# The first loads of a diffusion block in another order, the position table split, c turned with the filter's vectors

## What is computed

```
x  = x + pos_embed_2d(rows, GRID_W, D)            # table of 512 x 1024
mod = silu(c) @ w_mod + b_mod                     # 1024 -> 6144; the same with c_ctx for ctx
sh1, sc1, g1, sh2, sc2, g2 = split(mod, 6)
h  = rmsnorm(x, pre_norm1) * (1 + sc1) + sh1      # and hc from ctx with c_ctx
z  = h @ w_in                                     # Hyena group and mLSTM group
k  = hyena_filter(...)                            # 33 -> 64 -> 64 -> 64 -> 1024, sines between, times exp(-t*|delta|)
y_hy = x0 * irfft(rfft(v * x1) * rfft(k));  y_ml = two mLSTM scans, gates from h and hc
x  = x + g1 * rmsnorm([y_hy, y_ml] @ w_out)
x  = x + g2 * rmsnorm(experts(modulated rmsnorm of x))   # 16 experts, weights 3 x 8 MB each
```

## Time and profile before

| | us |
|---|---|
| median of 3 executions | 1326.48 (1326.43 to 1328.17) |
| the profiled execution | 1328.69 |
| its span, first to last instruction | 1326.6 |
| PE busy in the span | 1205.7 |
| start of hyena_tile(0) | 62.4 |
| end of hyena_tile(0) | 90.1 |
| first product of the experts | 401.8 |
| first wait of the experts for a transfer on the chain | 554.1 |

### The profile page before, as it was taken

The page is one execution under the profiler, slowest core; times in us unless marked ns, Lnnn a source line. Parts: engine busy times, 40 slices in busy tenths (PEclk is TensorE's granted clock), DMA queues, the critical chain, the costliest instruction groups (busy, mean ns, idle before and its releaser), DMA issues.

```text
span 1326.6 us, 12968 instructions
## 1 busy us (share of the span) xinstructions
PE 1205.7 (91%) x5284; PEld 500.9 (38%) x5284; DVE 351.7 (27%) x626; ACT 188.4 (14%) x392; POOL 30.6 (2%) x56
## 2 busy tenths in 40 slices
PE   5999999999989999998989798888979898897986
PEld 1444454654444353342325234232423422242332
DVE  3775729445450110210201111020102102010213
ACT  2510020134321111010101001010200101010012
POOL 2000020000000001000000000000000000000000
PEclk9999999999999999999999999999999999999999
DMA  9965410306168999999999999999999999999994
GB/s 348 387 230 222 143 64 0 127 1 253 66 258 371 390 428 429 427 427 428 428 428 429 429 428 428 428 429 429 429 427 428 429 428 429 427 429 428 428 427 168
DMA packets 44778, 455.57 MB, mean 343 GB/s; under 512 B 6193, under 2 KB 6305, under 8 KB 16971
## 3 DMA queue, kind: packets, MB, share of 16 engines
q1 hardware_dynamic: 44098, 454.95, 82.0%
q10 hardware_dynamic: 264, 0.11, 0.1%
q0 software_dynamic: 384, 0.07, 0.0%
HBM read 453.02 MB, written 2.10 MB: 343 GB/s over the span
## 4 chain that ended last, share of the span: by engine, by line
PE 59%; DMA 33%; DVE 5%; ACT 1%; issue 1%; SPq 1%; DVEq 0%; ACTq 0%
DMA ring<-in_w_exp_up 28%; PE B L1169 15%; PE B L1138 11%; PE B L720 6%; PE B L957 4%; PE B L1080 4%; PE B L841 3%; DMA ring<-in_w_exp_down 3%; PE B L899 2%; DMA ring<-in_pos 2%; PE B L1230 2%; PE B L770 2%; DVE moe L2058 1%; PE B L1151 1%; DVE yacc L2049 1%
## 5 line engine op out<-in xcount | busy, mean ns | idle before, releaser
L1138 PE MATMUL B<-ring,moe 128*64 128x512 f32 x2032 | 454.9, 596 | 75.5 <-DMA ring<-in_w_exp_up 41.5
L1138 PEld LDWEIGHTS B<-ring,moe 128*64 128x64 f32 x2032 | 139.2, 137 | 384.6 <-issue 247.5
L2058 DVE TENSOR_TENSOR moe<-moe,B 64x512 f32<-64x512 f32 x64 | 43.8, 685 | 700.4 <-PE B L1138 699.1
L1169 PE MATMUL B<-ring,moe 128*64 128x512 f32 x1008 | 222.1, 596 | 4.8 <-DMA ring<-in_w_exp_down 4.6
L1169 PEld LDWEIGHTS B<-ring,moe 128*64 128x64 f32 x1008 | 71.4, 137 | 144.0 <-issue 139.2
L1466 ACT ACTIVATE moe<-B 64x512 f32<-64x512 f32 x64 | 37.9, 592 | 413.8 <-PE B L1138 412.6
L720 PE MATMUL B<-ring 128*128 128x512 f32 x192 | 83.6, 594 | 0.0
L1230 PE MATMUL B<-moe 128*128 128x512 f32 x112 | 56.7, 618 | 4.5 <-DVE yacc L2049 4.1
L1080 PE MATMUL B<-moe,xl 128*128 128x128 f32 x448 | 55.0, 281 | 0.0
L1476 ACT ACTIVATE moe<-B 64x512 f32<-64x512 f32 x31 | 18.4, 592 | 252.5 <-PE B L1169 252.2
L1080 PEld LDWEIGHTS B<-moe,xl 128*128 128x128 f32 x448 | 53.9, 196 | 0.0
(11 more groups left out here) (339 smaller groups left out, 786.0 us busy)
## 6 DMA issues: line engine op xcount, KB each, us to landing
ring<-in_w_exp_up SPq DMA_DIRECT2D x64, 2048.0 KB, 31.8
ring<-in_w_exp_gate SPq DMA_DIRECT2D x63, 2048.0 KB, 30.4
ring<-in_w_exp_down SPq DMA_DIRECT2D x63, 2048.0 KB, 34.3
ring<-in_w_in SPq DMA_DIRECT2D x6, 2048.0 KB, 8.7
ring<-in_w_mod SPq DMA_DIRECT2D x10, 1024.0 KB, 7.6
ring<-in_w_mod SPq DMA_DIRECT2D x4, 2048.0 KB, 12.7
fr<-in_w_mod SPq DMA_DIRECT2D x6, 1024.0 KB, 9.1
ring<-in_w_out SPq DMA_DIRECT2D x2, 2048.0 KB, 7.9
```

The lines of the kernel that those rows point to most:

```text
L1138: x = mm(B[n][rows, :], xst[:, 2 * q + k, CAP * e2:CAP * (e2 + 1)], w[:, k, n * CH:(n + 1) * CH], start=(q == 0 and k == 0), stop=(q == 3 ...
L1169: x = mm(B[bank][CAP * half:CAP * (half + 1), :], src[:, q // 2, k * P + at:k * P + at + CAP], wd[:, k, half * CH:(half + 1) * CH], start= ...
L2058: v.tensor_tensor(hid[o, n // 2, :], sil[o, n // 2, :], B[n][o, :], ALU.mult).then_inc(S["v_hid"], 1)
```

## The change

- c and c_ctx move from `vr1` into `vr2`, are turned in a first transpose of 20 rows with the filter's vectors, and silu is made from an exponential ahead of layer 2 of the filter. The other small vectors (52 rows of `vr2`, `vr1`, `vr3`) are turned after the sixth tap.
- Of the constants only 260 of 852 columns are loaded first; `dl` is one row, spread over the partitions by a product on PE; the decays are made by ACT after the third sine.
- The position table is two tables: `pcol` (128 x 512) and `prow` (8 x 512, copied to 64 partitions at a time by two transfers).
- The order of loads is w_mod 0, x, positions, w_mod 1, ctx. Bytes moved into SBUF: 2.10 + 0.26 MB (`pos`, `dl`) become 0.26 + 1.05 MB, and 0.30 MB of the constants come behind w_mod 3: 1.35 MB fewer in front of w_mod 3, 1.05 MB fewer in all.
- `filter_spectrum(0)` comes before `mod_tile(1)`. The squares take x first and ctx last.
- The turned blocks of x come before all of those of ctx; ACT and DVE write four of them each into `ht`. The eight blocks of ctx are turned after group m = 0 of `hyena_tile(0)`, the gates come after group m = 1.

The diff, cut to this:

```diff
@@ sync
-            sp.dma_start(cst[:, :], A["cst"]).then_inc(d_cst, 16)
-            sp.dma_start(dlb, A["dl"]).then_inc(d_cst, 16)
...
+            for r, src in ((R_C, A["c"][0]), (R_CC, A["c_ctx"])):
+                sp.dma_start(vr2[r:r + 8, :], src.rearrange("(a b) -> a b", b=P)).then_inc(d_vec2, 16)
+            sp.dma_start(cst[:, 0:C_EARLY], A["cst"][:, 0:C_EARLY]).then_inc(d_cst, 16)
+            sp.dma_start(zft[0:FEMB, :], A["zft"]).then_inc(d_filt, 16)
+            sp.dma_start(fw1[0:FEMB, :], A["filt_w1"][0]).then_inc(d_filt, 16)
+            sp.dma_start(dlr[0:1, :], A["dl"]).then_inc(d_filt, 16)
+            for half in range(2):
+                sp.dma_start(fw2[FH * half:FH * (half + 1), :], A["filt_w2"][0]).then_inc(d_fw, 16)
...
+                if n == 1:
+                    sp.dma_start(x3, A["x"][0].rearrange("(c p) n -> p c n", p=P)).then_inc(d_x, 16)
+                    sp.dma_start(xn[:, 0, CH:D], A["pcol"]).then_inc(d_pos, 16)
+                    for r in range(2):
+                        sp.dma_start(xn[FH * r:FH * (r + 1), :, 0:CH],
+                                     A["prow"].rearrange("(c r) n -> r c n", r=2)[r].partition_broadcast(FH)).then_inc(d_pos, 16)
                 if n == 2:
                     sp.dma_start(cx, A["ctx"][0].rearrange("(c p) n -> p c n", p=P)).then_inc(d_ctx, 16)
-                    sp.dma_start(x3, A["x"][0].rearrange("(c p) n -> p c n", p=P)).then_inc(d_x, 16)
-                    sp.dma_start(xn, A["pos"].rearrange("(c p) n -> p c n", p=P)).then_inc(d_pos, 16)
                 if n == 4:
+                    sp.dma_start(cst[:, C_EARLY:C_COLS], A["cst"][:, C_EARLY:C_COLS]).then_inc(d_gate, 16)
@@ tensor
+            def rows_of_context(k):
+                b = [n for n in range(3, 8) if n != hy_bank[0]][k % 4]
+                take(b)
...
+                users[b] = (S["v_htc"], k + 1)
+
+            pe.wait_ge(S["v_xn"], NTT)
+            for k in range(3):
+                rows_of_latents(k)
             mod_turn(0, 1)
...
+            for k in range(3, KD):
+                rows_of_latents(k)
...
             def hyena_tile(i, between=None):
...
+                    if m == 0 and i == 0:
+                        for c in range(KD):
+                            rows_of_context(c)
+                    if m == 1 and i == 0:
+                        gates()
...
+            pe.wait_ge(S["a_htl"], KD // 2)
+            pe.wait_ge(S["v_htl"], KD // 2)
             hyena_tile(0)
@@ scalar
             filter_odd(1)
-            for t in range(NCT, NTT):
-                squares(t)
+            squares(2)
+            squares(3)
             filter_odd(2)
+            act.wait_ge(d_ctx, 16)
+            squares(4)
+            squares(5)
             act.wait_ge(S["a_ss"], NTT)
@@ vector
+            for k in range(1, KD, 2):
+                dve.wait_ge(S["p_htl"], k + 1)
+                v.tensor_scalar(ht[:, k, LC:], B[htl_bank[k]][:, :], aff1[:, 0, 0, k:k + 1],
+                                aff1[:, 0, 1, k:k + 1], ALU.mult, ALU.add).then_inc(S["v_htl"], 1)
```

More of the change, by code:

```diff
@@ L101, in tiles @@
             m.reshape(w, rows // P, P, cols).transpose(2, 0, 1, 3).reshape(P, w * rows // P * cols).astype(np.float32))
-    return {"cst": cst, "pos": pe, "zft": zft, "dl": dl, "dft": tiles(fwd), "idft": tiles(inv)}
+    return {"cst": cst, "pcol": pcol, "prow": prow, "zft": zft, "dl": dl, "dft": tiles(fwd), "idft": tiles(inv)}
 def step_of(d, tile):
@@ L568, in upper @@
                 return ident[0:m, 0:m]
-            pe.wait_ge(d_cst, 32)
+            pe.wait_ge(d_cst, 16)
             pe.wait_ge(d_vec2, 16 * N_VEC2)
[L573 to L604, removed]
+            tr(B[1][:, 0:R2_EARLY], vr2[0:R2_EARLY, :], upper(R2_EARLY)).then_inc(S["p_vt"], 1)
             def weights(kind, i):
@@ L672, in spectrum, with filter_layer, tap @@
                     users[b] = (odd_used if odd else even_used, n + 1)
+            def filter_layer(n):
+                for half in range(2):
+                    r = slice(FH * half, FH * (half + 1))
+                    if n == 0:
+                        w, src = fw1[0:FEMB, :], zft[0:FEMB, half * LC:(half + 1) * LC]
+                    else:
+                        w, src = (fw2, fw3)[n - 1][r, :], fh[r, :]
+                    x = mm(B[4][r, (n % 2) * LC:(n % 2 + 1) * LC], w, src, start=True, stop=True)
+                x.then_inc(S["p_fil"], 1)
+            def tap(n):
+                w, c = TAPS[n]
+                b = 4 + n % 4
+                r = slice(FH * (c // 2), FH * (c // 2 + 1))
+                if n >= 4:
+                    pe.wait_ge(S["v_kf"], n - 3)
+                mm(B[b][:, :], fh[r, (c % 2) * P:(c % 2 + 1) * P], fws[r, w, :], start=True, stop=True)\
+                    .then_inc(S["p_kf"], 1)
+                users[b] = (S["v_kf"], n + 1)
+            pe.wait_ge(d_filt, 48)
+            filter_layer(0)
+            mm(B[3][:, :], cst[0:1, C_ONE:C_ONE + P], dlr[0:1, :], start=True, stop=True).then_inc(S["p_vt"], 1)
+            users[3] = (S["a_dec"], NLT)
+            pe.wait_ge(d_fw, 64)
+            pe.wait_ge(S["a_fil"], 1)
+            filter_layer(1)
+            pe.wait_ge(S["a_fil"], 2)
+            filter_layer(2)
+            pe.wait_ge(S["v_fws"], 2)
+            pe.wait_ge(S["a_fil"], 3)
+            for n in range(6):
+                tap(n)
+            pe.wait_ge(d_vec1, 16 * N_VEC1)
+            tr(B[0][:, 256:256 + R2_ROWS], vr2[0:R2_ROWS, :], upper(R2_ROWS))
+            tr(B[0][:, 0:R1_ROWS], vr1[0:R1_ROWS, :], upper(R1_ROWS))
+            tr(B[0][:, 128:140], vr3[0:12, 0:2 * P:2], upper(12))
+            tr(B[0][:, 140:152], vr3[0:12, 1:2 * P:2], upper(12)).then_inc(S["p_vt"], 1)
+            users[0] = users[1] = (S["v_vt"], 2)
+            tap(6)
+            tap(7)
             pe.wait_ge(S["v_cpad"], 1)
             mod_tile(0)
-            mod_tile(1)
             def filter_spectrum(n):
@@ L684, in _ @@
             filter_spectrum(0)
+            mod_tile(1)
             pe.wait_ge(S["v_kf"], len(TAPS))
@@ L704, in _, with rows_of_latents @@
[L704 to L713, removed]
+            def rows_of_latents(k):
+                b = next_bank()
+                htl_bank[k] = b
+                for c in range(NLT):
+                    x = tr(B[b][:, c * P:(c + 1) * P], xn[:, c, k * P:(k + 1) * P], idn)
+                x.then_inc(S["p_htl"], 1)
+                users[b] = (S["v_htl"] if k % 2 else S["a_htl"], k // 2 + 1)
@@ new lines, in _, with gates @@
+            for k in range(3, KD):
+                rows_of_latents(k)
+            def gates():
+                pe.wait_ge(S["v_htc"], KD)
+                pe.wait_ge(d_gate, 48)
+                take(0)
+                for k in range(KD):
+                    for n in range(3):
+                        x = mm(B[0][32 * n:32 * n + 16, 0:LC], wgate_sb[:, k, :], ht[:, k, n * LC:(n + 1) * LC],
+                               start=(k == 0), stop=(k == KD - 1))
+                x.then_inc(S["p_gt"], 1)
+                users[0] = (S["a_gt"], 3)
@@ L1308, in _ @@
             act.wait_ge(S["v_kf"], len(TAPS))
-            for k in range(KD):
+            for k in range(0, KD, 2):
                 act.wait_ge(S["p_htl"], k + 1)
```

146 lines of the change are left out of this document (69 added, 77 removed).

## The result

| | before | changed |
|---|---|---|
| median, us (runs of one job) | 1326.45 (1326.38 to 1328.17, 4) | 1336.27 (1335.43 to 1337.19, 4) |
| profiled execution, us | 1328.69 | 1336.06 |
| its span, us | 1326.6 | 1334.1 |

The ratio is 1.0069, with a 95% interval of 1.0057 to 1.0081. The change makes the kernel slower, by 7.6 to 10.7 us. The forecast was 3 us, with a range that ended at 1331.4.

The account below looks back on a forecast made before the run. PE was taken to bound the kernel ahead of 554 us, then the experts' transfers, moving with the front. +1.65 us for mod_turn(0)'s start and +1.4 behind it gave +3.05: 1329.5 us against the median 1326.48, range 1325.4 to 1331.4.

Parts of the forecast that it names:

- PE in front of mod_tile(1) at 32.1: After mod_tile(0) and filter_spectrum(0), PE would be ready for mod_tile(1) at 32.1 us, bounds 30.2 and 33.8.
- dft at 14.85: The dft load, behind ten more issues, would land 2.0 us later than before, at 14.85.
- The price of prow, 4.2 us: In the load queue, prow's two 64-partition transfers would take 4.2 us at 249 GB/s, so w_mod 1 lands at 34.65.
- The upper bound of the landing: Latest landing of w_mod 1: 34.65 us or a little more, the 64-fold read of prow's rows being unpriced.
- The clock: Rival, chance 0.10: PE falls to 1.2 GHz at the start of hyena_tile(0), +1.5 to +1.7 us, total 1331.2.
- T = mod_tile(1) + 18.3: T, the start of mod_turn(0), would come 18.3 us after mod_tile(1) starts, at 53.0, 1.65 later than before.
- Behind T +1.4: From mod_turn(0) to the end of hyena_tile(0): 38.72 - 5.8 + 3.64 + 3.5 = 40.1 us, 1.4 longer.
- DVE's row tiles at nothing: DVE's row tiles start some 8 us later but cost nothing, the eighth having been ready 9.9 us early.
- the experts one for one: The second part, from 554 us on, with the experts' transfers, would move one for one with the front.
- full rate: Rival, chance 0.25: prow moves at 415 GB/s or dft lands no later; +1.2 us, total 1327.7.
- w_mod 1 isn't late: Rival, chance 0.10: w_mod 1 lands at 31 with PE already there; -0.65 us, total 1325.8.
- More than I see: Rival, chance 0.10: starting hyena_tile(0) at 58.3 instead of 62.4 is worth its 4 us.

Follow-up runs that it names:

- e2: Changed kernel with prow written out to 512 rows and loaded by one transfer of 128 partitions; 1329.65 us, ratio 1.0020 to before.
- e6: e2 with the stretch behind mod_turn(0) as before the change, except that DVE still counts the modulation's halves apart; 1327.24 us, ratio 1.0002 to before.
- e7: e2 with the ctx blocks turned four after group m = 0 and four after m = 1, gates after m = 2; 1327.59 us, ratio 0.9997.
- e3: Changed kernel with prow written out to 512 rows, still loaded by two transfers of 64 partitions; 1336.31 us, ratio 1.0063 to before.
- e5: Changed kernel with six extra unread products on PE between filter_spectrum(0) and mod_tile(1); 1334.08 us, ratio 1.0049 to before.
- e4: The kernel before the change, unchanged, profiled a second time; 1327.88 us, ratio 1.0005 to before.
- e1: Changed kernel with w_mod 1 loaded ahead of x and the positions, as before the change; 1333.61 us, ratio 1.0050 to before.

## Why the prediction was wrong

The direction was right, and so was the path: mod_tile(1) waits for a w_mod 1 made late by the strips of prow, and PE stands in the tile for banks. But two terms were wrong, one too small and one missing. Step by step, in its own order:

- **PE in front of mod_tile(1) at 32.1.** It was 31.8. mod_tile(0) came at 25.03 for 25.2. Right.
- **dft at 14.85.** It landed at 14.4, w_mod 0 at 19.4 for 19.85. Right.
- **The price of prow, 4.2 us: this step failed.** From the landing of w_mod 0 to that of w_mod 1 the sum had 5.0 + 0.6 + 4.2 + 5.0 = 14.8 us; it took 37.4 - 19.4 = 18.0. With pcol landed at 26.4 and the table at 32.6, the table alone shows 6.2 us, and x ahead of it took 6.4 from the landing of w_mod 0. In e2, e6 and e7, where only the form of the table differs in the loads, x took 5.1 to 5.2, so the strips slow their neighbour too. If all the excess is put down to prow, its price is 7.4 us. I had taken 249 GB/s from the earlier trace rows as the rate of such transfers, but in that window dft, in full width, was also on its way (it landed at 12.84), so the row gave no rate of strips alone. The upper bound of the landing, "34.65 or a little more", was therefore no bound. The Trainium skill, page "SBUF — State Buffer", section "Door 1: The DMA port swizzle", has half the ports and about 218 GB/s for 64 partitions. The windows of 165 to 256 lie around that, so the trace agrees with it in size. With its 4.8 us the landing would have been an estimate of 35.2, still 2.2 early: the table took 1.4 more than this and x 1.4 more than its 5.0, and dft and w_mod 1 came 0.6 sooner than the sum had them. e2 shows that it is the form of the load, and e3 that it is not the repeated read; the width is what is left, if the number of transfers costs nothing. How the DMA engines share their time between a strip and a full transfer no run here measures.
- **The clock: this step failed.** The prediction weighed a fall at the start of hyena_tile(0), at 0.10, and kept 1.00 for mod_tile(1). It had written itself that PE would stand from 32.1 to 34.65, and didn't ask what that does. The wait was 5.60 and the price 1.72 on mod_tile(1). Whether the wait of 2.55 that it forecast would have cost the clock, no run shows: those measured are 1.13 to 1.72, with the full clock behind them, and 3.58 to 7.04, with half. At hyena_tile(0) nothing fell: its first sixteen products take 7.10 or 7.11 in every run with the new stretch, and before's 64 take 27.66. e5 shows the cost and the cause.
- **T = mod_tile(1) + 18.3.** It is 19.85 in the change, 1.55 more by the clock, and 18.04 to 18.08 in e5, e6 and e7, where it didn't fall. Right but for the clock. T was to be 53.0 and is 57.26: 2.76 from the landing, 1.55 from the clock.
- **Behind T +1.4.** It is +0.97. The tile starts 4.84 after T, not 5.25. DVE's writes set it: the first comes 1.77 after T, and the four take 2.97, not 3.35. ACT starts 1.30 after T and not 1.89, because `v_aff` now counts the two halves of the modulation apart. I had read over that in the diff; it is off the path here. The stop for the banks is 3.11, not 3.5. Against these two savings of 0.4 each, the tile's 64 products, now in pieces, take 28.17 and not 27.66, a term that the sum didn't have. Right in kind, 0.4 too dear; e7 shows that it is this stop which makes the new stretch longer than the old.
- **DVE's row tiles at nothing, the experts one for one.** Both right: cover 9.9 as before, and the first expert's wait moved by 7.16.
- **The account against the median.** I took the 2.2 us by which the profile of before lies over its median as the same on both sides. The change's profile lies 0.2 under its own median. So the profiles differ by 1336.06 - 1328.69 = 7.4 and the medians by 9.8. e4 shows 1.0 of the difference, the half-clock spell at its first modulation tiles. Against e4 the end of the tile moved by 96.95 - 89.04 = 7.9 us, which is inside the interval of 7.6 to 10.7. The last 1.9 up to the medians' difference is not settled. Another spell at half the clock, between 400 and 460, is in both profiles alike (granted clock 0.97 there) and missing in e1 and e6 (1.00), and four runs don't tell how often it comes. Medians of the kernel before itself are 1326.45, 1326.63, 1327.55, 1327.80 and 1327.88, the second and the last in one job, so 1.3 us between medians of one kernel is not unusual.

Of the rivals, "full rate" and "w_mod 1 isn't late" are excluded by the first windows; the clock was the right rival at the wrong place. "More than I see" did not occur.

## What to carry to other kernels

A load's byte count says little until its shape is known: the same 1 MB cost 6.6 us more when it was written in two strips of 64 partitions than in one transfer of 128, and the strips slowed the transfer beside them too. When a wait is forecast for TensorE, ask what it does to the clock behind it, at the place of the wait. When an early load is made late, look for the next one in the queue before you move it back: e1 gained 5.5 us at one wait, and T gained only 0.7, since the row table then came later.

## What of the hardware I had not expected

- Two transfers of 64 partitions and 512 KB each hold not only themselves back: with the DMA engines busy at 1.06 to 1.16 of their time, all queues together moved 165 to 256 GB/s from 24 to 30 us (the change and e3), and x, of full width, landed 6.4 and 7.4 us behind w_mod 0; with the table in 128 partitions (e2) it was 410 to 422 GB/s and 5.2 us.
- Reading each source row 64 times cost nothing that shows; writing the table out made it no faster (e3).
- Waits of TensorE of 3.58 us (e2), 4.74 (e1), 5.60 (the change) and 7.04 (e3) were followed by a modulation tile of 3.44 to 3.64 us, waits of 1.13 (e6), 1.69 (e4) and 1.72 (e7) by one of 1.92.
- SP needed 1.38 and 2.47 us to issue the two strips, and 0.36 to 0.51 for dft, w_mod 0, x and pcol ahead of them. The width is not the reason: w_mod 1, of 128 partitions, took 3.88 behind the strips, and 5.94 in e2, where there are none. Late in the row of issues they are all long; what holds them no run here settles.
